# Two transformer layers on one core: a new start, and attention norms and rotary sums moved in the engines' queues

## The reference

```
for i in range(DEPTH):                       # DEPTH = 2
    h = rms_norm(x, attn_norm[i])
    x = x + (fox_mixer if i == 0 else swa_mixer)(h, ...)
    h = rms_norm(x, ffn_norm[i])
    x = x + conv_glu_ffn(h, ffn_w_up[i], ffn_conv_w[i], ffn_conv_b[i], ffn_w_down[i])
fox_mixer: q, k, v, f = split(h @ w_in)      # 16 heads of 128
    q, k = rms_norm per head; c = cumsum(log_sigmoid(f + f_bias))
    p = softmax(q k^T / sqrt(128) + (c_i - c_j), causal); out = (p v) @ w_out
swa_mixer: q, k, v = split(h @ w_in)         # 32 query heads, 4 key heads of 64
    q, k = rope(rms_norm per head)           # x1*cos - x2*sin, x2*cos + x1*sin
    banded softmax with a sink, in chunks of 64 tokens; out = (p v) @ w_out
conv_glu_ffn: gate, up = split(h @ w_up)     # 5632 each
    out = (silu(causal_conv_3(gate) + bias) * up) @ w_down
```

## Time and profile before

| | |
|---|---|
| median of 3 runs | 2131.58 us |
| the profiled execution | 2130.38 us |
| its span | 2128.6 us |
| PE busy | 2108.3 us (99%) |
| DVE busy, ACT busy | 1299.0 us (61%), 1010.4 us (47%) |
| DMA | 390.69 MB, mean 184 GB/s |
| chain that ended last, by engine | PE 93%, DVE 3%, ACT 1%, issue 1%, DMA 1% |

### The profile page before, as it was taken

How to read it: one execution, slowest core, us unless ns; L and a number is a source line. 1 busy time by engine, 2 the same in 40 slices (tenths; PEclk the granted TensorE clock), 3 DMA queues, 4 the chain that set the end, 5 groups by cost and what they waited for, 6 DMA issues and landing times.

```text
span 2128.6 us, 29755 instructions
## 1 busy us (share of the span) xinstructions
PE 2108.3 (99%) x10844; PEld 1798.4 (84%) x10844; DVE 1299.0 (61%) x1560; ACT 1010.4 (47%) x1329; POOL 3.9 (0%) x9
## 2 busy tenths in 40 slices
PE   7999999999999999999999999999999999999999
PEld 6788888888888888888888788888888888888887
DVE  5655565566766667654445677566667666664443
ACT  5545555444444444444444556544444444443332
POOL 0000000000000000000000000000000000000000
PEclk9999999999999999999999999999999999999999
DMA  7665565666666666666666544566666666666665
GB/s 227 208 176 163 164 176 173 185 188 187 178 196 178 197 188 178 196 194 190 190 190 194 172 130 128 170 186 188 188 188 178 196 188 182 195 192 192 193 193 165
DMA packets 206249, 390.69 MB, mean 184 GB/s; under 512 B 12844, under 2 KB 17756, under 8 KB 206172
## 3 DMA queue, kind: packets, MB, share of 16 engines
q1 hardware_dynamic: 203440, 387.25, 61.1%
q10 hardware_dynamic: 2732, 2.39, 0.3%
HBM read 387.48 MB, written 2.11 MB: 183 GB/s over the span
## 4 chain that ended last, share of the span: by engine, by line
PE 93%; DVE 3%; ACT 1%; issue 1%; DMA 1%; ACTq 0%; DVEq 0%
PE ps L1115 44%; PE ps L1105 31%; PE ps L1111 16%; DMA bt<-c_rows 1%; PE ps L1211 1%; DVE wlo L830 1%; ACT whi L558 0%; DVE qtok L918 0%; ACT sqj L642 0%; PE ps L1261 0%; DVE ssh L909 0%; PE ps L1289 0%; DVE mxs L1004 0%; PE ps L1272 0%; PE ps L1280 0%
## 5 line engine op out<-in xcount | busy, mean ns | idle before, releaser
L830 DVE TENSOR_TENSOR wlo<-raw,whi 128x1024 fp32r<-128x1024 f32 x376 | 459.5, 1225 | 449.7 <-ACT whi L558 449.4
L1105 PE MATMUL ps<-hs,whi 128*128 128x512 f32 x2832 | 709.2, 392 | 0.0
L558 ACT ACTIVATE whi<-raw 128x1024 fp32r<-128x1024 f32 x378 | 399.6, 1060 | 511.8 <-PE ps L1115 503.2
L836 DVE TENSOR_TENSOR wlo<-raw,whi 128x1024 fp32r<-128x1024 f32 x352 | 425.5, 1223 | 282.4 <-ACT whi L565 282.2
L565 ACT ACTIVATE whi<-raw 128x1024 fp32r<-128x1024 f32 x352 | 371.4, 1061 | 468.6 <-PE ps L1111 468.5
L1105 PEld LDWEIGHTS ps<-hs,whi 128*128 128x128 f32 x2832 | 509.6, 189 | 91.2
L1111 PEld LDWEIGHTS ps<-hs,wlo 128*128 128x128 f32 x2816 | 384.2, 190 | 27.5
L1111 PE MATMUL ps<-hs,wlo 128*128 128x256 f32 x2816 | 392.6, 282 | 0.0
L1115 PE MATMUL ps<-whi,gs 128*128 128x512 f32 x1408 | 348.6, 389 | 0.0
L1115 PEld LDWEIGHTS ps<-whi,gs 128*128 128x128 f32 x1408 | 263.9, 188 | 54.6
L1115 PE MATMUL ps<-whi,hs 128*128 128x512 f32 x1088 | 279.1, 399 | 2.1 <-ACT whi L558 2.0
(11 more groups left out here) (143 smaller groups left out, 868.3 us busy)
## 6 DMA issues: line engine op xcount, KB each, us to landing
raw<-in_ffn_w_up SPq DMA_DIRECT2D x352, 512.0 KB, 3.7
raw<-in_ffn_w_down SPq DMA_DIRECT2D x176, 512.0 KB, 4.7
raw<-in_fox_w_in SPq DMA_DIRECT2D x98, 512.0 KB, 3.9
raw<-in_swa_w_in SPq DMA_DIRECT2D x40, 512.0 KB, 3.7
raw<-in_fox_w_out SPq DMA_DIRECT2D x32, 512.0 KB, 4.6
raw<-in_swa_w_out SPq DMA_DIRECT2D x32, 512.0 KB, 3.9
xk<-in_x SPq DMA_DIRECT2D x8, 256.0 KB, 6.5
bt<-c_rows ACTq DMA_DIRECT2D x1, 2048.0 KB, 15.8
```

The costliest lines, as they stand in the source:

```text
L558: act.activation(whi[slot][:, :], raw[slot][:, :], ACT.Copy).then_inc(hi_ready, 1)
L830: tt(wlo[slot][:, :], raw[slot][:, :], whi[slot][:, :].bitcast(F32), ALU.subtract).then_inc(lo_ready, 1)
L836: tt(wlo[slot][:, :], raw[slot][:, :], whi[slot][:, :].bitcast(F32), ALU.subtract).then_inc(lo_ready, 1)
L1105: return pe.matmul(ps[:, bank, :], whi[slot][:, c:c + P], moving.rearrange("p h t -> p (h t)"), start=first, stop=last)
```

## The change

The kernel's lines after the change have other numbers than before (L830 has become L836, L1115 has become L1125, and so on).

1. Start, PE: `WARM` = 11 products of a constant tile into an unused bank before the first wait, and `FILL` = 4 more behind the first transposes of x. The constant `ones_t` is set first on DVE.
2. Start, transfers: ACT's queue keeps the identity and the first pair of gains; the second pair and the convolution weights (five DMAs) are issued by SP behind the sixth weight unit. The second pair of gains is transposed and copied at step `tab`.
3. Start, preparation: `prep(0, 0)` in two halves, each in front of the conversion of the unit that needs it.
4. `sum`, `rcol` and `stats` of the first norm come at steps 5, 6 and 8 and no longer at 4, 5 and 5.
5. The head norms' `sq`, `rd` and `qn` stand in front of the conversion that they stood behind; `ln` keeps its place.
6. `spread` in two DMAs: heads 0 to 3, then heads 4 to 15 with a semaphore of their own, which later `bm` steps wait for.
7. `wr2` right behind `wr1`.

```diff
+WARM = 11
+FILL = 4
...
-                new = {7: [("sq", m), ("rd", m), ("ln", m), ("qn", m)],
+                front = {7: [("sq", m), ("rd", m), ("qn", m)], 15: [("sq", m + 1), ("rd", m + 1), ("qn", m + 1)]}
+                new = {7: [("ln", m)],
...
-                       15: [("sq", m + 1), ("rd", m + 1), ("ln", m + 1), ("qn", m + 1)],
+                       15: [("ln", m + 1)],
...
-                         4: [("tab", 0), ("sum", 0)], 5: [("rcol", 0), ("stats", 0)],
+                         4: [("tab", 0)], 5: [("sum", 0)], 6: [("rcol", 0)],
...
-                         8: [("gain", 0)], 10: [("f1", 0)], 11: [("f2", 0)], 12: [("send", 0)], 14: [("spread", 0)]}
+                         8: [("gain", 0), ("stats", 0)], 10: [("f1", 0)], 11: [("f2", 0)], 12: [("send", 0)], 14: [("spread", 0)]}
...
+                        steps += front.get(i, [])
                         steps.append(("unit", fox_unit(24 * p + i), "QKV"[i // 8], p, i % 8))
...
-                    chain += {0: [("wsq", c), ("wrd", c)], 1: [("wln", c), ("wqn", c)], 2: [("wr1", c)], 3: [("wr2", c)],
+                    chain += {0: [("wsq", c), ("wrd", c)], 1: [("wln", c), ("wqn", c)], 2: [("wr1", c), ("wr2", c)],
...
+            sp.dma_start(grow[:, 2:4, :], ffn_norm.rearrange("l (k p) -> k l p", p=P)).then_inc(c_land, 16)
+            for l in range(LAYERS):
+                sp.dma_start(small[:, 4 * l:4 * l + 3, :], ffn_conv_w[l].rearrange("j (f p) -> f j p", p=P)).then_inc(c_land, 16)
+                sp.dma_start(small[:, 4 * l + 3, :], ffn_conv_b[l].rearrange("(f p) -> f p", p=P)).then_inc(c_land, 16)
...
-            for n, g in enumerate((attn_norm, ffn_norm)):
-                act.dma_start(grow[:, 2 * n:2 * n + 2, :], g.rearrange("l (k p) -> k l p", p=P)).then_inc(g_land, 16)
-            for l in range(LAYERS):
...
+            act.dma_start(grow[:, 0:2, :], attn_norm.rearrange("l (k p) -> k l p", p=P)).then_inc(g_land, 16)
...
-                    act.dma_start(bt[:, :, 1:3, :].rearrange("p h a c -> p h (a c)"),
...
+                    for h0, h1 in ((0, 4), (4, FOX_H)):
+                        act.dma_start(bt[:, h0:h1, 1:3, :].rearrange("p h a c -> p h (a c)"),
+                                      c_rows[h0:h1, :].rearrange("h t -> (h t)").partition_broadcast(P)
+                                      .rearrange("p (h t) -> p h t", h=h1 - h0)).then_inc(b_land if h0 == 0 else b_rest, 16)
...
             act.wait_ge(v_tab, 1)
-            prep(0, 0)
+            prep(0, 0, (0, 1))
             conv_hi(0, 0)
+            prep(0, 0, (2, 3))
             conv_hi(1, 1)
...
                     dve.wait_ge(b_land, 2 * 16)
+                    if n:
+                        dve.wait_ge(b_rest, 16)
...
-            prep(0, 0)
+            prep(0, 0, (0, 1))
             conv_lo(0)
+            prep(0, 0, (2, 3))
             conv_lo(1)
...
-                    pe.wait_ge(c_land, 4 * 16)
+                    pe.wait_ge(c_land, 5 * 16)
+                    for m in range(2):
+                        pe.transpose(ps[:, 6, 8 * FT + m * KT:8 * FT + (m + 1) * KT], grow[:, 2 + m, :], ident[0:KT, 0:KT])
...
+            pe.wait_ge(v_set, 1)
+            for m in range(WARM):
+                pe.matmul(ps[:, 3, P * (m % 4):P * (m % 4) + P], ones_t[:, 0:P], ones_t[:, P:T], start=True, stop=True)
             pe.wait_ge(i_land, 16)
-            pe.wait_ge(g_land, 2 * 16)
-            for m in range(2 * LAYERS):
+            pe.wait_ge(g_land, 16)
+            for m in range(2):
...
             transposes(0, 0)
+            for m in range(FILL):
+                pe.matmul(ps[:, 3, P * (m % 4):P * (m % 4) + P], ones_t[:, 0:P], ones_t[:, P:T], start=True, stop=True)
```

More of the change, by code:

```diff
@@ L241, in trunk @@
         b_land = sem("b_land")
+        b_rest = sem("b_rest")
         v_bm = sem("v_bm")
@@ L545, in _ @@
             act.dma_start(ident[:, :], cs("ident")).then_inc(i_land, 16)
-            for n, g in enumerate((attn_norm, ffn_norm)):
-                act.dma_start(grow[:, 2 * n:2 * n + 2, :], g.rearrange("l (k p) -> k l p", p=P)).then_inc(g_land, 16)
-            for l in range(LAYERS):
-                act.dma_start(small[:, 4 * l:4 * l + 3, :],
-                              ffn_conv_w[l].rearrange("j (f p) -> f j p", p=P)).then_inc(c_land, 16)
-                act.dma_start(small[:, 4 * l + 3, :], ffn_conv_b[l].rearrange("(f p) -> f p", p=P)).then_inc(c_land, 16)
+            act.dma_start(grow[:, 0:2, :], attn_norm.rearrange("l (k p) -> k l p", p=P)).then_inc(g_land, 16)
             def conv_hi(u, slot):
@@ L580, in square_x, with prep @@
                 last.then_inc(a_ss, 1)
-            def prep(n, g):
-                for q in range(4):
+            def prep(n, g, part=range(4)):
+                for q in part:
                     k = 4 * g + q
@@ L629, in step @@
                     act.wait_ge(b_land, 16)
-                    act.dma_start(bt[:, :, 1:3, :].rearrange("p h a c -> p h (a c)"),
-                                  c_rows.rearrange("h t -> (h t)").partition_broadcast(P)
-                                  .rearrange("p (h t) -> p h t", h=FOX_H)).then_inc(b_land, 16)
+                    for h0, h1 in ((0, 4), (4, FOX_H)):
+                        act.dma_start(bt[:, h0:h1, 1:3, :].rearrange("p h a c -> p h (a c)"),
+                                      c_rows[h0:h1, :].rearrange("h t -> (h t)").partition_broadcast(P)
+                                      .rearrange("p (h t) -> p h t", h=h1 - h0)).then_inc(b_land if h0 == 0 else b_rest, 16)
                 elif kind == "sq":
@@ L870, in step @@
                     dve.wait_ge(p_tab, 2)
+                    dve.tensor_copy(gains[:, 2:4, :], ps[:, 6, 8 * FT:8 * FT + 2 * KT].rearrange("p (n k) -> p n k", k=KT))
                     dve.tensor_copy(conv[:, :, :, :], ps[:, 6, 0:8 * FT].rearrange("p (l w f) -> p l w f", l=LAYERS, w=4)).then_inc(v_tab, 1)
@@ L1070, in ffn @@
                     step(s)
+            dve.memset(ones_t[:, :], 1.0).then_inc(v_set, 1)
             for free in (v_gate, v_up, v_tap, v_glo):
@@ L1077, in _ @@
             dve.memset(gbuf[:, :, 0:2], 0.0).then_inc(v_set, 1)
-            dve.memset(ones_t[:, :], 1.0).then_inc(v_set, 1)
             dve.memset(fb[96:128, :], 0.0).then_inc(v_set, 1)
@@ L1082, in _ @@
             dve.wait_ge(p_tab, 1)
-            dve.tensor_copy(gains[:, :, :], ps[:, 2, 0:4 * KT].rearrange("p (n k) -> p n k", k=KT)).then_inc(v_tab, 1)
-            prep(0, 0)
+            dve.tensor_copy(gains[:, 0:2, :], ps[:, 2, 0:2 * KT].rearrange("p (n k) -> p n k", k=KT)).then_inc(v_tab, 1)
+            prep(0, 0, (0, 1))
             conv_lo(0)
+            prep(0, 0, (2, 3))
             conv_lo(1)
```

## The result

The kernel before took 2131.89 us (median of 4 runs, 2131.50 to 2133.47), the changed one **2117.44 us** (4 runs, 2117.09 to 2117.61): ratio 0.9926, interval 0.9914 to 0.9938. The profiled execution took 2117.55 us, its span is 2115.7, against 2130.38 and 2128.6.

The account below looks back on a forecast made before the run. PE was taken as the bound, busy 2108.3 of 2128.6 us. Terms 3.6 + 2.6 + 1.5 + 1.1 + 2.4 = 11.2 took the profiled 2130.38 to 2119.2, median 2120.4; 8-in-10 range 2118.0 to 2125.0.

Parts of the forecast that it names:

- The step from execution to median: End of the sum: the median of the runs lies 1.2 us above the profiled execution, so 2119.2 becomes 2120.4.
- Head norms: Norms of head blocks moved ahead of a conversion: all seven PE waits go, 1.5 us won, bounds 0 to 1.5.
- rival 4: Norms in front starve the weight pipeline through late raw buffers and loads, making the kernel slower: 2136, chance 0.02.
- Rotation: Rotation's sum right behind its products: 2.4 us of PE's waits won, 0.6 stays in the second chunk; bounds 1.5 to 3.0.
- rival 3: Rotation's sum in front delays the softmax chain; probabilities come late in three chunks, half of 2.4 us lost: 2121.6, chance 0.06.
- Start: Kernel start up to unit 1: unit 0 begins at 9.2 at full rate (2.76 us); 3.6 us won, bounds 2.0 to 4.3.
- This is what is late next: At the start, unit 0's raw data, landing at 8.1 us, were to be what holds up its conversion.
- First norm: First norm's products: PE's 2.18 us wait and their slow standing start go, 2.6 us won, bounds 0 to 2.6.
- Bias: Score bias split into two transfers: PE's wait of 1.1 us goes, the first quarter taking 4 to 8 us; bounds 0 to 1.1.
- Rival 1: At the start, the gap ahead of unit 0 drops the clock or warming fails: 1.6 us less won, 2122.0, chance 0.15.
- the forecast's own bound of 2118.8: Fast end of the forecast itself, reached with earlier landings at the start and the rotation's whole 3.0 us won.

Follow-up runs that it names:

- the second trace of before: The kernel before, with no edit, run again for a second profiled execution: 2134.44 us.
- part 4 alone: The kernel before with only the first norm's sum, rcol and stats moved to steps 5, 6 and 8: 2129.00 us, beside 2132.59 for the kernel before.

## Why the forecast was wrong

The direction was as forecast, every wait that was to go went, and no rival came true as it was priced. Wrong were the last step of the sum, from one execution to the median, and the price of short waits: "The profiled execution took 2130.38 and would take 2119.2; the median of the runs is 1.2 higher, 2131.58, and becomes 2120.4." Of the 2.96 us between 2120.4 and 2117.44, 1.65 lie in the terms and 1.3 in that last step; either of the two put right moves the range's lower end of 2118.0 below the measured time.

- **The step from execution to median** failed. The 1.2 was taken as a constant and was part of what the change removes: a unit 0 that becomes fast later (5.46 for 4.33), a fall of the clock behind the stall (7.06 for 5.48) and a longer bias wait, all three in the second trace of before and not in the first. The changed kernel has neither the cold unit 0 nor the stall, and its profiled execution lies 0.1 from its median. For the fall it is shown: part 4 alone is worth 3.6 by medians and 2.3 at equal clock. How much unit 0 adds in the median is not known; its first eight products took 3.42, 3.58 and 3.75 us in the three traces with the old start.
- **Head norms** (1.5, measured 3.1 by starts, 2.8 by undoing) is the term most mis-sized. Seven rows of idle time were summed as they stand, and their sum was taken for the upper bound ("Bounds 0 to 1.5"); a wait costs 0.35 to 0.5 where the row shows 0.2 to 0.3. The price of a late low part was rightly put at nothing for seven of the norms. At the first, the load did come late (rival 4's mechanism), in the changed kernel still under cover by some tenths.
- **Rotation** (2.4, measured 3.0): the same mis-reading, 3.25 for five rows of 3.0 less the 0.6 that stayed; less 0.22 at `oT`. The softmax chain was held up as rival 3 says, but at one wait for `oT` and not at the probabilities, for 0.22 and not 1.2.
- **Start** (3.6, measured 2.90): unit 0 at 9.59, not 9.2, near its forecast rate (3.01 in the chain for 2.76). "This is what is late next" named the data, wrongly for this trace: unit 0's data landed at 7.8, and ACT came to them only at 8.39, since the four first transposes took 0.94 us at the slow pace. By the durations the 2.4 GHz rate arrived only in the transposes, after 22 passes of warming at 0.23 us each. Part of the miss is the execution: eight other traces with this start have unit 0 at 9.04 to 9.58.
- **First norm** (2.6, measured 2.37): right.
- **Bias** (1.1, measured 1.46): above its bound of 1.1, a short wait priced by its row again, and wrong in attribution. Either part 5 or part 6 wins it alone; the first 512 KB took 7.7 us, within the bounds given.
- **Rival 1** did not happen with the filling products (0.70 us of idle time, where the forecast had 1.3) and did without them. Without the warming products unit 0 was slow too, but from a clock that had not risen.
- **A slip in the bounds:** the two gains named for the forecast's own bound of 2118.8 add up to 1.3, which gives 2119.1.
- **What stays open**: why the clock falls behind 1.59 us of idle time and not behind 1.43 (filling products stood in front of the second, so the two differ in more than length), and behind 2.2 in some executions only; and why the kernel without warming spreads over 1.35 us with a clock of 1.000 throughout. For this last the two traces of before offer a reading that was not tested: the moment at which a cold unit 0 becomes fast moves by 1.1 us, and the granted clock does not show it.

## What to carry to other kernels

Before terms are added up, look at how the runs of the kernel spread and at what its profiled execution shows against them: where a gap makes later work slow in some executions, the gain of closing it is its idle time plus the slow work's share, and the median moves more than a lucky trace says. Count a short wait of PE as its row plus some 0.2 us. And an engine's order sets the issue of loads several units on: a late buffer can be a price (the raw load at 42 us) or a present (the bias transfer undisturbed), so undo parts in pairs before a gain is given to one of them. And look at the duration of a load as well as its issue before an edit is blamed for a new wait.

## What the hardware showed that was not expected

- The clock fell behind 1.59 us of idle time that followed transposes, and behind 2.2 us in one trace of before (a mean of 0.83 in the window shown above) and not in the other. Both times the one unit that followed took 1.6 us longer. It did not fall in the traces with 0.70 and 1.43 us of idle time behind the filling products.
- Products of 128 columns from 1.2 us on ran at 0.23 us a pass for 5 us; the same form took 0.13 a pass at 7.84. In another trace (part 7 undone) the same 22 passes took 4.19 us and not 5.06, so the moment at which the rate rises moves by about a microsecond. The granted clock reads 1.00 in these first microseconds all the same; only the durations show the slow start.
- One 2048 KB broadcast took 12.6 us where a 512 KB weight load was issued 8.3 us after it, and 15.8, 15.9, 16.3 and 16.7 in four traces where that load came after 5.0 us; its first quarter alone took 7.7, not a quarter of that.
- The same 512 KB weight load, issued between 41 and 44 us, took 3.9 to 4.1 us in eight traces and 5.1 and 5.2 in two.
